# Two feed-forward up products a pair, as seven block products with Strassen's scheme instead of eight

## The reference, cut

```python
# first layer
h = rms_norm(x, ffn_norm_g[l]) * (1 + scale_f) + shift_f
u, v = jnp.split(h @ w_up[l], 2, axis=-1)
u = causal_depthwise_conv(u, conv_w[l], conv_b[l])
x = x + gate_f * ((jax.nn.silu(u) * v) @ w_down[l])
# second layer
u = rms_norm_2(h, ffn_pre_g)
f = jax.nn.silu(jnp.einsum('bsd,df->bsf', u, w_ffn_gate)) * jnp.einsum('bsd,df->bsf', u, w_ffn_up)
h = h + rms_norm_2(jnp.einsum('bsf,fd->bsd', f, w_ffn_down), ffn_post_g)
```

## Time and profile before

| | |
|---|---|
| three runs, median (lowest to highest) | 2914.85 us (2912.55 to 2921.71) |
| the profiled execution | 2915.09 us, its span 2911.5 us |
| granted TensorE clock, mean | 0.957 |
| PE busy in the span | 2720.7 us, 93% |
| DVE, ACT, POOL busy | 1225.3, 584.3, 1086.9 us |
| first feed-forward stage | about 691 to 1422 us |
| second feed-forward stage | about 2146 to 2878 us |

### The profile page before, as it was taken

How to read it: one execution, slowest core, us unless ns; L and a number is a source line. 1 busy time by engine, 2 the same in 40 slices (tenths; PEclk the granted TensorE clock), 3 DMA queues, 4 the chain that set the end, 5 groups by cost and what they waited for, 6 DMA issues and landing times.

```text
span 2911.5 us, 32355 instructions
## 1 busy us (share of the span) xinstructions
PE 2720.7 (93%) x12448; PEld 2245.3 (77%) x12448; DVE 1225.3 (42%) x1410; ACT 584.3 (20%) x943; POOL 1086.9 (37%) x500
## 2 busy tenths in 40 slices
PE   6899988798999999999899999999979999999995
PEld 5777778776888888888687877777868888888884
DVE  6454238735333333333766045446362222222225
ACT  3122435412111100010312044431230000000001
POOL 2422245433434434434644322222434344334432
PEclk8999887899999999999999999999999999999998
DMA  6322000111111111111211100002101111111111
GB/s 248 121 96 86 29 29 0 58 37 36 44 50 50 43 50 50 44 49 50 98 43 36 51 30 29 33 32 87 51 22 44 50 50 43 50 50 46 47 50 58
DMA packets 35182, 158.39 MB, mean 54 GB/s; under 512 B 4032, under 2 KB 4288, under 8 KB 32448
## 3 DMA queue, kind: packets, MB, share of 16 engines
q1 hardware_dynamic: 32976, 139.60, 13.4%
q10 hardware_dynamic: 2160, 18.16, 1.6%
HBM read 149.35 MB, written 8.39 MB: 54 GB/s over the span
## 4 chain that ended last, share of the span: by engine, by line
PE 82%; issue 7%; DVE 6%; ACT 2%; POOL 2%; DMA 1%; POOLq 0%; ACTq 0%; DVEq 0%; SPq 0%
PE ps L460 21%; PE ps L464 21%; PE ps L461 21%; PE ps L495 4%; PE ps L497 4%; PE ps L496 4%; PE ps L829 1%; PE ps L667 1%; PE ps L855 1%; PE ps L609 1%; DVE ada_acc L1276 1%; POOL xw L443 1%; DVE sq L1616 1%; DMA ada_first<-ada 1%; PE ps L622 1%
## 5 line engine op out<-in xcount | busy, mean ns | idle before, releaser
L378 POOL TENSOR_TENSOR w_hi<-raw,ones 128x1024 fp32r<-128x1024 f32 x210 | 414.6, 1974 | 1663.7 <-PE ps L464 1205.0
L460 PE MATMUL ps<-h_hi,w_hi 128*128 128x512 f32 x2016 | 792.4, 393 | 24.1 <-DVE h_lo L1250 12.2
L461 PE MATMUL ps<-h_lo,w_hi 128*128 128x512 f32 x2016 | 789.2, 391 | 0.0
L464 PE MATMUL ps<-h_hi,w_lo 128*128 128x512 f32 x2016 | 623.9, 391 | 0.0
L381 POOL TENSOR_TENSOR w_lo<-raw,w_hi 128x1024 fp32r<-128x1024 f32 x210 | 540.4, 2573 | 16.5
L460 PEld LDWEIGHTS ps<-h_hi,w_hi 128*128 128x128 f32 x2016 | 381.7, 189 | 108.8 <-issue 18.9
L461 PEld LDWEIGHTS ps<-h_lo,w_hi 128*128 128x128 f32 x2016 | 381.7, 189 | 78.8
L464 PEld LDWEIGHTS ps<-h_hi,w_lo 128*128 128x128 f32 x2016 | 380.7, 189 | 79.9
L460 PE MATMUL ps<-act_hi,w_hi 128*128 128x512 f32 x704 | 275.5, 391 | 5.8 <-DVE act_lo L1563 5.8
L461 PE MATMUL ps<-act_lo,w_hi 128*128 128x512 f32 x704 | 275.0, 391 | 0.0
L1559 DVE TENSOR_TENSOR act_f<-silu_u,ps 128x1024 f32<-128x1024 f32 x44 | 53.7, 1221 | 507.1 <-PE ps L464 506.0
(11 more groups left out here) (279 smaller groups left out, 2883.5 us busy)
## 6 DMA issues: line engine op xcount, KB each, us to landing
raw<-wstream SPq DMA_DIRECT2D x210, 512.0 KB, 3.2
ada_rest<-ada SPq DMA_DIRECT2D x8, 2048.0 KB, 7.7
ada_first<-ada SPq DMA_DIRECT2D x8, 1024.0 KB, 24.5
xw<-x_t SPq DMA_DIRECT2D x2, 2048.0 KB, 13.5
xw<-x_t ACTq DMA_DIRECT2D x1, 4096.0 KB, 13.1
x_spill<-xw ACTq DMA_DIRECT2D x1, 4096.0 KB, 11.8
xw<-x_spill ACTq DMA_DIRECT2D x1, 4096.0 KB, 12.2
out<-xw ACTq DMA_DIRECT2D x8, 512.0 KB, 2.6
```

The lines of the kernel that those rows point to most:

```text
L378: pool.tensor_tensor(w_hi[s][:, :], raw[s][:, :], ones[:, :].broadcast_to([P, 1024]), ALU.mult).then_inc(w_split, 1)
L460: pe.matmul(ps_out[:, sl], w_hi[s][:, wsl], hi[:, first_k + k, sl], start=a, stop=False)
L461: pe.matmul(ps_out[:, sl], w_hi[s][:, wsl], lo[:, first_k + k, sl], start=False, stop=False)
L464: mm = pe.matmul(ps_out[:, sl], w_lo[s][:, wsl], hi[:, first_k + k, sl], start=False, stop=z)
```

## The change

U0, U1 and V0, V1 are the two halves (over 512 input channels each) of the weights of a u tile and a v tile, B11, B12 (upper half of the channels) and B21, B22 (lower half) the blocks of h for the left and the right half of the tokens. Before, eight block products give u and v. Now there are seven, in Winograd's form of Strassen's scheme, with T1 = B12 - B11, T3 = B22 - B12, T2 = B22 - T1, T4 = B21 - T2 made once a stage, and S1 = V0 + V1, S2 = S1 - U0, S3 = U1 - S2, S4 = U0 - V0 made for each pair. One block product is 12 matmuls (four 128x128 blocks, three matmuls each).

- POOL makes the differences of h (`combine_h`) and the sums of weights (`sum_first`, `sum_third`, `sum_last`), and the low parts of all weight blocks of the two stages (`block_low`).
- ACT makes the high parts of the weight blocks (`block_high`, called by `raw_high` and `sum_high`) and of the seven blocks of h (`combine_split`). Its pair-wise work is in `pair_turns`; `take` starts the convolution or takes Silu, `silu` the Silu behind the convolution.
- A weight block (128x512, high and low) lies in one of three ring slots, four at the start of a stage. Raw units have three slots, loaded by SP in `load_ffn` from a second tensor, `wffn`.
- PE accumulates in PSUM banks (`pair`): an x bank takes the first, third, fifth and seventh product, the y bank the second and fourth, the z bank the sixth. Since the partial sums are shared between outputs, ACT copies the bank out between products (`snap`: to the left of `u_s`, to `v_right`, to the right of `u_s`), and DVE adds the other banks to these copies (`join_right`, `join_low`, `join_left`). The left half of v stays in the x bank.
- u is now in SBUF (`u_s`) when the convolution reads it, and the product with v is made in two halves, the right one of two SBUF tiles.
- In the first pair of a stage three products are worked along with the making of h; the other four wait for all of it.
- `y_acc` now lies over x in the second stage. So x is written to memory (`x_keep`) behind the squares and read back (`x_end`) during the last down products, and `y_acc` is cleared behind the second pair.

```diff
+B11, T1, B21, B22, T3, T2, T4 = range(7)
+PRODUCTS = (B11, T1, T2, B22, T3, B21, T4)
+FIRST_PRODUCTS = (B11, T1, B21, T2, B22, T3, T4)
...
+    combos = [at("combos_a", [P, 4, 2, KK, HALF], F32R, A0), wk("combos_b", [P, 3, 2, KK, HALF], F32R, 0)]
+    h_pair = [[wk(f"h_pair{j}{q}", [P, T], F32, 48 + 8 * j + 4 * q) for q in range(2)] for j in range(2)]
+    h_diff = [wk(f"h_diff{j}", [P, 3, HALF], F32, 64 + 6 * j) for j in range(2)]
+    u_s = wk("u_s", [P, T], F32, 64)
+    v_right = wk("v_right", [P, HALF], F32, 72)
+    w_sum = [xk(f"w_sum{j}", [P, HALF], F32, 112 + 2 * j) for j in range(2)]
+    ring = [[at(f"ring{n}_{q}", [P, HALF], F32R, (8 + 4 * m) * K + 2 * K * q) for q in range(2)]
+            for n, m in enumerate((2, 1, 0, 3))]
...
+        def combine_h(ph, shifted):
+            made = (lambda kk: pool.wait_ge(h_shifted, 2 * kk + 2)) if shifted else (
+                lambda kk: pool.wait_ge(nrm_scaled, 2 * KD + 2 * kk + 2))
+            for kk in range(KK):
+                top, low = h_pair[kk % 2]
+                d = h_diff[kk % 2]
+                n = 4 * (KK * ph + kk)
+                made(kk)
+                if kk >= 2:
+                    pool.wait_ge(combo_ready, COMBOS * ph + 3 * (kk - 1))
+                pool.tensor_tensor(d[:, 0, :], half(low, 1), half(top, 1), ALU.subtract).then_inc(h_differed, 1)
+                pool.wait_ge(h_differed, n + 1)
+                pool.tensor_tensor(half(top, 1), half(top, 1), half(top, 0), ALU.subtract).then_inc(h_differed, 1)
+                pool.wait_ge(h_differed, n + 2)
+                pool.tensor_tensor(d[:, 1, :], half(low, 1), half(top, 1), ALU.subtract).then_inc(h_differed, 1)
+                pool.wait_ge(h_differed, n + 3)
+                pool.tensor_tensor(d[:, 2, :], half(low, 0), d[:, 1, :], ALU.subtract).then_inc(h_differed, 1)
+        def block_low(b, slot, src):
+            pool.wait_ge(blk_hi, b + 1)
+            pool.tensor_tensor(ring[slot][1][:, :], src, ring[slot][0][:, :].bitcast(F32),
+                               ALU.subtract).then_inc(blk_ready, 1)
...
+        def pair_blocks(b, p, u, v, u_ready, v_ready, slots):
+            sum_first(b, p, u, v, u_ready, v_ready)
+            block_low(b, slots[0], half(raw_f[u], 0))
+            block_low(b + 1, slots[1], w_sum[0][:, :])
+            sum_third(b + 2, p, u)
+            block_low(b + 2, slots[2], w_sum[1][:, :])
+            sum_last(p, u, v)
+            block_low(b + 3, slots[3], w_sum[0][:, :])
+            block_low(b + 4, slots[4], half(raw_f[v], 0))
+            block_low(b + 5, slots[5], half(raw_f[u], 1))
+            block_low(b + 6, slots[6], half(raw_f[v], 1))
...
-            def up(t, k, unit):
-                pe.wait_ge(w_split, 2 * unit + 2)
-                unit_tile(ps[2 * t + k], k, KD, 0, h_hi, h_lo).then_inc(unit_done, 1)
+        def product_tiles(dst, slot, blk, kk, start, stop):
+            wsl = slice(kk * P, (kk + 1) * P)
+            pe.matmul(dst, ring[slot][0][:, wsl], combo(blk, 0)[:, kk, :], start=start, stop=False,
+                      skip_group_check=True)
+            pe.matmul(dst, ring[slot][0][:, wsl], combo(blk, 1)[:, kk, :], start=False, stop=False,
+                      skip_group_check=True)
+            return pe.matmul(dst, ring[slot][1][:, wsl], combo(blk, 0)[:, kk, :], start=False, stop=stop,
+                             skip_group_check=True)
+        def product(b, dst, slot, blk, start):
+            pe.wait_ge(blk_ready, b + 1)
+            for kk in range(KK):
+                mm = product_tiles(dst, slot, blk, kk, start and kk == 0, kk == KK - 1)
+            mm.then_inc(blk_used, 1)
+        def pair(b, p, t, slots, after_first=False):
+            xb = x_bank[t]
+            for j, (dst, blk) in enumerate(zip((xb, y_bank, xb, y_bank, xb, z_bank, xb), PRODUCTS)):
+                if j == 0 and not after_first:
+                    pe.wait_ge(f_act, p - 1)
+                elif j == 1:
+                    pe.wait_ge(joined, 3 * p if after_first else 3 * p - 2)
+                elif j in (2, 3, 4):
+                    pe.wait_ge(snapped, 3 * p + (j - 1))
+                elif j == 5:
+                    pe.wait_ge(joined, 3 * p)
+                elif j == 6:
+                    pe.wait_ge(joined, 3 * p + 2)
+                product(b + j, dst, slots[j], blk, j in (0, 1, 5))
...
+            first_pair_products(ph)
+            pair(b + 7, p + 1, 1, [j % 3 for j in range(7)], after_first=True)
             with pe.Fori(1, FG) as i:
-                pe.wait_ge(f["act"], 2 * i - 1)
-                for k in range(2):
-                    up(0, k, 6 * i + (u0 + k - 2))
-                down(i, 6 * i + u0)
-                for k in range(2):
-                    pe.wait_ge(f["dn_free"], 8 * i + (k - 1))
-                    up(1, k, 6 * i + (u0 + 2 + k))
-            last_down(u0 + 6 * FG - 2)
-        ffn_phase(ffn[0], U_FFN1, H_N1)
+                pair(18 * i + (b - 4), 2 * i + p, 0, [(1 + j) % 3 for j in range(7)])
+                down(i, 18 * i + (b + 3))
+                pair(18 * i + (b + 7), 2 * i + (p + 1), 1, [j % 3 for j in range(7)])
+            last_down(b + BLOCKS - 4)
...
+            def pair_turns(bp, pair, t, u, v, ready_v, ready_u, slots, prev=None, high=None):
+                xb, yb = (half(ps[0], 0), half(ps[1], 1))[t], half(ps[0], 1)
+                sum_high(bp + 2, slots[2], pair, 2, w_sum[1][:, :], bp)
+                u_free(pair)
+                snap(half(u_s, 0), xb, bp + 1)
+                sum_high(bp + 3, slots[3], pair, 3, w_sum[0][:, :], bp + 1)
+                if prev is not None:
+                    silu(prev)
+                    act.wait_ge(f_act, pair)
+                snap(v_right[:, :], yb, bp + 2)
+                sum_high(bp + 4, slots[4], pair, 4, half(raw_f[v], 0), bp + 2)
+                snap(half(u_s, 1), xb, bp + 3)
+                raw_high(bp + 5, slots[5], u, 1, ready_u, bp + 3)
+                if prev is not None:
+                    act_high(prev, 1 - t)
+                raw_high(bp + 6, slots[6], v, 1, ready_v, bp + 4)
...
+        def combine_split(ph, n, src, gain):
+            def lows(kk):
+                for run, (hi, lo, whole) in enumerate(zip(combo_runs(kk, 0), combo_runs(kk, 1), combo_sources(kk))):
+                    dve.wait_ge(combo_hi, COMBOS * ph + 3 * kk + run + 1)
+                    dve.tensor_tensor(lo, whole, hi.bitcast(F32), ALU.subtract).then_inc(combo_ready, 1)
+            dve.wait_ge(rb_ready, INV_RUN[n] + 1)
+            for kk in range(KK):
+                if kk >= 2:
+                    dve.wait_ge(combo_ready, COMBOS * ph + 3 * (kk - 1))
+                for q in range(2):
+                    dve.scalar_tensor_tensor(h_pair[kk % 2][q][:, :], src[:, kk + KK * q, :], gain(kk + KK * q),
+                                             ps[NORM_BANK[n]][:, :], ALU.mult, ALU.mult).then_inc(nrm_scaled, 1)
+                if kk:
+                    lows(kk - 1)
+            lows(KK - 1)
...
+            def join_low(pair, t, count):
+                dve.wait_ge(snapped, 3 * pair + 2)
+                dve.wait_ge(blk_used, count)
+                dve.tensor_tensor(v_right[:, :], v_right[:, :], (half(ps[0], 0), half(ps[1], 1))[t],
+                                  ALU.add).then_inc(joined, 1)
...
+            def product(pair, t, count):
+                dve.wait_ge(f_silu, pair + 1)
+                dve.wait_ge(blk_used, count)
+                dve.wait_ge(joined, 3 * pair + 3)
+                dve.tensor_tensor(half(act_f, 1), half(act_f, 1), v_right[:, :], ALU.mult)
+                dve.tensor_tensor(half(act_f, 0), half(act_f, 0), (half(ps[0], 0), half(ps[1], 1))[t],
+                                  ALU.mult).then_inc(f_act, 1)
...
+            def segment(bp, pair, t, prev):
+                product(prev, 1 - t, bp)
+                join_right(pair, bp + 4)
+                low(prev, 1 - t)
+                join_low(pair, t, bp + 5)
+                join_left(pair, bp + 6)
+                convolve(pair)
```

525 lines of the change are left out of this document (374 added, 151 removed).

## The result

The changed kernel takes 2865.07 us in the median of four runs (2862.38 to 2867.25), the kernel before beside it 2913.70; the ratio is 0.9828, with a 95% interval of 0.9806 to 0.9849, so 1.7% less, clear of the noise. The forecast was 2864 us, its range 2840 to 2902. Of the runs further on, one of e4_two_v (4437.0 us, clock 0.552) and one of e5_swap_two_v (3304.86 us, clock 0.754) were slow and are left out of their medians and ratios. The profiled execution has a span of 2865.2 us against 2911.5.

A forecast was written before the change was run, and what follows sets the result against it. PE was taken to bound the kernel, time being matmuls times their spacing. Against 2915.09 us, -119.8 + 57.2 + 4.4 + 1.8 + 8 - 2.9 = -51.3 gave 2864 us, range 2840 to 2902.

The forecast's parts named there:

- Matmuls removed: Both feed-forward stages: 528 matmuls fewer at an unchanged spacing of 0.2269 us, -119.8 us on PE's path.
- The starts: Start of each stage: PE idles while POOL, ACT and DVE make the blocks of h; +30.7 and +26.5 us.
- The step: One of four steps making h's blocks at a stage start: 10.35 us in stage 1, 9.1 in stage 2.
- PE cold: After each start's idle, about 11 matmuls at the lower clock in front of full work; +4.4 us (0 to 6).
- The join of v_right: First pair of each stage: the seventh product waits for DVE's join; 0.9 us twice, +1.8 us.
- The loop: Stage with the convolution: v_right and POOL's third block come late, 0.8 us an iteration, +8 us; stage 2, 0.
- Clearing y_acc: Behind the second pair: the 6.9 us clearing ends 1.5 us before it would be late; uncovered, it costs once.
- The ends: Ends of the stages: PE's wait for act_lo is covered in stage 2, -2.9 us; stage 1, 0.
- bound by the chain: Rival: fixed orders of ACT, DVE and POOL add 1.0 to 2.5 us an iteration; 2876 to 2906 us, 19%.
- the fewer matmuls: Rival: PE's saving is eaten by the starts or by wider matmul spacing; 2905 to 2923 us, 4%.
- The clock did not fall: Rival: PE's short stops in nearly every pair lower the clock, up to 114 us over 44 pairs, 2978 us; 7%.

The follow-up runs named there:

- e4_two_v: Changed kernel with two v_right buffers, one for even and one for odd pairs; 2855.59 us, ratio 0.9795 to the kernel before.
- e5_swap_two_v: Changed kernel with two v_right buffers and POOL's low part of the third weight block ahead of sum S3; 2856.05 us, ratio 0.9791.
- e1_fewer: Kernel before with 12 of each pair's 96 matmuls left out (v incomplete), 504 fewer in all; 2805.17 us, ratio 0.9614.
- e7: Changed kernel with the first of POOL's four differences of each step at the stage starts made twice; 2877.47 us, ratio 0.9862.
- e10: Changed kernel with ACT adding the shift to the next step's h before the last copy, first stage; 2863.38 us, ratio 0.9816.
- e8: Changed kernel with the first difference of each step (T3) made by DVE, not POOL; 2860.30 us, ratio 0.9802.
- e3: Changed kernel with POOL making the low part of a pair's third weight block before sum S3, not behind it; 2883.50 us, ratio 0.9890.
- e11: e4_two_v with ACT making the next even pair's second block's high part before the odd pair's convolution; 2847.77 us, ratio 0.9773.

## Why the prediction was right

**Matmuls removed**, -119.8: right, by e1_fewer to 0.2 us in 57.

**The starts**, +57.2: stage 1 lost 20.2 of its 59.9, so 39.7 was added; less the loop (9 intervals of 0.82, and 1.2 in the pair ahead of them) and the join (0.85), the start cost 30.3 against 30.7. Stage 2: 26.3 added, less 0.85 and 1.3, 24.2 against 26.5. The step was walked as 10.35 and 9.1 and is 9.86 and 8.61; POOL's 512 took 1.27 where I took 1.30, and POOL came in 4.3 and 3.4 behind the first scaling and not 4.9. The last combos are ready 43.4 and 38.7 us behind the scaling (forecast 45.7 and 41.9). The price came from the right places: POOL's chain (e7), the shift (e10), and the turns with DVE, which the rows show and e8 did not test by themselves.

**PE cold**, +4.4: wrong, it was nearly 0. The changed kernel, stage 1:

```profile
735.46 0.63 PE L894 MATMUL ps<-combos_a,ring 128*128 128x512 f32 x1
735.88 0.45 PE L890 MATMUL ps<-combos_a,ring 128*128 128x512 f32 x1
...
737.60 0.50 PE L890 MATMUL ps<-combos_b,ring 128*128 128x512 f32 x1 [0.80 <-DVE combos_b L1595]
737.93 0.40 PE L892 MATMUL ps<-combos_b,ring 128*128 128x512 f32 x1
```

The slow matmuls, 0.43 apart, belong to the last step and lie in front of a wait; the clock has risen to 2.4 GHz by the time that PE has work without end. The step that failed: I took the 11 slow matmuls to come behind the last wait.

**The join of v_right**, +1.8: 0.85 twice, right.

**The loop**, +8: right, 60.66 against 59.84, 0.82 an iteration where 0.8 was said, and 0 in stage 2. The two places were the right ones as well, the third block and the v_right copy. That they were two paths of nearly the same length, and that S3 stands in one, I had not seen; it cost e3's expectation.

**The second and third pair.** Clearing y_acc was to end 1.5 us before it would be late: PE waits 1.31 once, since DVE starts the 6.88 us at 2203.94, 1.66 behind the join ahead of it, and the product with v begins behind them at 2211.26. The slack was wrong by 2.8. In stage 1's second pair PE waits 1.18, also unforeseen: POOL waited 4.75 for a unit to land, and ACT loads Silu's table there for 1.28.

**The ends.** Stage 2, -2.9: -3.2 to the sums, then +2.7 to the end in this execution: PE had waited 3.97 for the sums of squares (2.45 before), and sums and spread ran partly at 1.2 GHz (granted clock 0.63 from 2829 to 2842 us), the spread taking 3.67 where it took 1.99. Over the eleven executions of the changed kernel and its variants, that last stretch is 31.0 to 35.4, the two shortest with two partials; two cases don't prove a cause. Stage 1, 0: wrong by 4.8. I had read PE's own wait before the down products, which did stay (2.93 against 2.88 in the earlier trace rows), and not when the first output is done, which POOL's queue behind it passes on.

**The rivals.** The loop is not bound by the chain at 1.0 us or more, and the fewer matmuls are paid in full. The clock did not fall: 1.00 in both loops, though PE stops twice in every even pair of the first, for about 0.3 us each. The Trainium skill's rule (TensorE: Matmul & The Clock Gate, "A second HAM failure mode: psum-queue depth-cycling") did not show here. But the rival was no empty one. In e3_third_first, where PE stops for 1.88 us once an iteration, the clock did fall behind three of ten stops, at some 1.6 us each.

So the sum was 2864 for 2865, with misses that cancel: 7.1 too much at the starts with the cold clock, 2.5 too little in the second and third pairs, 4.8 at the end of stage 1, and 5.9 in this execution's stretches that the change leaves alone (1.0 too much lies in the loop, the join and the end of stage 2, and 1.8 around the span, 2867.01 being this execution's own time). The large terms were right for their reasons; that the sum came within 1 us is luck.

## What to carry to other kernels

When a scheme trades multiplications for additions, price the additions where nothing covers them: the matmuls were worth 119.8 us and the sums beside the loops cost 8, but the two starts cost 54.5. Before a wait is taken away, list every path that ends at the same place: here two were nearly equally late, and repairing one gained 0.12 of 0.82 us an iteration, repairing both all of it. Where work is passed on output by output, look at when the first output is done, not only at how long PE waits (this one is read from rows here, not tested).

## What the runs showed that I had not expected

- Moving an operation of two SBUF inputs from POOL to DVE (1.27 to 0.69 us alone) made a step of stage 2 longer, 8.61 to 9.34, mostly by the place that it took in DVE's order.
- Behind a wait of 1.88 us in a full loop the granted clock was 0.53 for some seven matmuls in three cases of ten, and not in the others (e3).
- One statement's place in ACT's program was worth 6.3 us (e11, on top of e4) and 4.2 us (e10), and the place of one in POOL's cost 18.8 us (e3), with no work added or removed.
- Stretches that no edit touches differ between executions by up to 13 us (685.3 to 698.7 us to the first scaling), while an iteration of the changed kernel's loop repeats to 0.05 us.
